# Low parts of the weights in four GpSimd instructions per tile, in every stage

## What is computed

```python
h = _rmsnorm(x, norm_mix)
z = h @ w_in
xr, gr, q, k, v, iq, ik, iw, ga, gb = jnp.split(z, _split_points(), axis=-1)
xc, new_buf = _causal_conv(xr, conv_buf, conv_w, conv_b)
yr, h_last = _rg_lru(xc, h0, w_rg_a, b_rg_a, w_rg_x, b_rg_x, lam)
branch_a = (yr * jax.nn.gelu(gr)) @ w_rnn_out
o = attend(q, k, v, iq, ik, iw)          # top-k keys by the indexer
branch_b = o.reshape(B, T, ATT_W) @ w_att_out
x = x + (jax.nn.sigmoid(ga) * branch_a + jax.nn.sigmoid(gb) * branch_b) @ w_o
h2 = _rmsnorm(x, norm_ffn)
x = x + (jax.nn.silu(h2 @ w_ffn_gate) * (h2 @ w_ffn_up)) @ w_ffn_down
h3 = _rmsnorm(x, norm_ple)
x = x + jax.nn.sigmoid(h3 @ w_ple_gate) * (p_l @ w_ple_proj)
```

## Time and profile before

| | |
|---|---|
| median of three runs | 1089.46 us |
| the profiled execution | 1090.71 us |
| its span, first to last instruction | 1089.0 us |
| TensorE busy | 1038.4 us (95%) |
| VectorE busy | 454.9 us (42%) |
| ScalarE busy | 406.2 us (37%) |
| GpSimd busy | 450.5 us (41%) |
| of it, wlo (line 1512, 213 instructions) | 383.5 us |
| chain that ended last, TensorE's share | 89% |
| mean granted TensorE clock | 0.979 |

### The profile page before, as it was taken

One profiled execution on the slowest core, in us unless ns is written; L12 is line 12 of the kernel. 1 busy time (PEld: TensorE's weight loads), 2 busy tenths in 40 slices (PEclk: granted clock), 3 DMA queues, 4 the chain that ended last, 5 costly groups with the idle time before them and its releaser, 6 DMA issues.

```text
span 1089.0 us, 19209 instructions
## 1 busy us (share of the span) xinstructions
PE 1038.4 (95%) x7847; PEld 977.2 (90%) x7847; DVE 454.9 (42%) x715; ACT 406.2 (37%) x690; POOL 450.5 (41%) x307
## 2 busy tenths in 40 slices
PE   4879999999998999999999899999999999999897
PEld 3867998777897888989999899999999999999796
DVE  3315899487896443423433422222000222212653
ACT  5424233556675443333332622222112222222634
POOL 2613441164665455334441543433444333344540
PEclk9898999999998999999999899999999999999899
DMA  6643265324222312333252323222333232132402
GB/s 181 178 75 90 65 181 152 119 69 145 74 64 77 92 41 69 98 83 94 79 170 69 116 79 96 77 82 68 91 102 104 86 88 69 55 88 80 117 1 82
DMA packets 168750, 101.97 MB, mean 94 GB/s; under 512 B 12626, under 2 KB 160754, under 8 KB 168418
## 3 DMA queue, kind: packets, MB, share of 16 engines
q1 hardware_dynamic: 168674, 100.91, 32.9%
HBM read 93.26 MB, written 7.63 MB: 93 GB/s over the span
## 4 chain that ended last, share of the span: by engine, by line
PE 89%; DVE 4%; ACT 2%; DMA 2%; issue 1%; POOL 1%; SPq 1%; ACTq 0%; DVEq 0%
PE psD L1727 78%; PE psX L1682 2%; DMA wraw<-in_w_in 1%; PE held L1936 1%; PE held L1682 1%; PE psX L1992 1%; PE held L1880 1%; PE psX L1923 1%; PE held L2016 1%; PE psX L1810 1%; DVE h_lo L1063 1%; DMA prm<-in_state_rglru_h 1%; ACT whi L606 1%; DVE hs L1265 0%; DVE xc L1133 0%
## 5 line engine op out<-in xcount | busy, mean ns | idle before, releaser
L1512 POOL TENSOR_TENSOR wlo<-wraw,whi 128x1024 fp32r<-128x1024 f32 (+5 forms) x213 | 383.5, 1812 | 575.8 <-ACT whi L606 575.8
L1727 PE MATMUL psD<-h_hi,whi 128*128 128x272 f32 (+1 forms) x1616 | 348.4, 297 | 13.5 <-DVE h_lo L1063 10.4
L1727 PE MATMUL psD<-h_lo,whi 128*128 128x272 f32 (+1 forms) x1616 | 339.1, 292 | 0.0
L1727 PE MATMUL psD<-h_hi,wlo 128*128 128x272 f32 (+1 forms) x1616 | 339.1, 292 | 0.0
L1727 PEld LDWEIGHTS psD<-h_hi,whi 128*128 128x128 f32 (+1 forms) x1616 | 258.5, 192 | 33.3 <-issue 23.6
L1727 PEld LDWEIGHTS psD<-h_lo,whi 128*128 128x128 f32 (+1 forms) x1616 | 259.3, 192 | 0.0
L606 ACT CAST whi<-wraw 128x1024 fp32r<-128x1024 f32 (+4 forms) x165 | 154.9, 939 | 277.5 <-PE psD L1727 250.2
L1727 PEld LDWEIGHTS psD<-h_hi,wlo 128*128 128x128 f32 (+1 forms) x1616 | 257.3, 192 | 0.0
L1727 PE MATMUL psD<-act_hi,whi 128*128 128x272 f32 x672 | 140.8, 291 | 0.0
L1727 PE MATMUL psD<-act_hi,wlo 128*128 128x272 f32 x672 | 139.1, 288 | 0.0
L1727 PE MATMUL psD<-act_lo,whi 128*128 128x272 f32 x672 | 138.7, 288 | 0.0
(11 more groups left out here) (262 smaller groups left out, 948.6 us busy)
## 6 DMA issues: line engine op xcount, KB each, us to landing
wraw<-in_w_in SPq DMA_DIRECT2D x48, 512.0 KB, 4.9
wraw<-in_w_ffn_gate SPq DMA_DIRECT2D x22, 512.0 KB, 3.7
wraw<-in_w_ffn_up SPq DMA_DIRECT2D x22, 512.0 KB, 3.8
wraw<-in_w_ffn_down SPq DMA_DIRECT2D x16, 384.0 KB, 3.4
wraw<-in_w_ffn_down SPq DMA_DIRECT2D x16, 320.0 KB, 3.2
kpg<-in_cache_k SPq DMA_DIRECT2D x16, 256.0 KB, 3.0
kpg<-in_cache_v SPq DMA_DIRECT2D x16, 256.0 KB, 3.3
wraw<-in_w_rnn_out SPq DMA_DIRECT2D x8, 512.0 KB, 4.8
```

The lines of the kernel that those rows point to most:

```text
L1512: ins = g_.tensor_tensor(wlo[:, s, r0:r1, 0:cc], wraw[:, s, r0:r1, 0:cc], whi[:, s, r0:r1, 0:cc].bitcast(F32), ALU.subtract)
L1727: ins = te.matmul(psD[0:cc, b0 + half, 0:HT], w[:, s, c, 0:cc], m[:, k0 + c, HT * half:HT * (half + 1)], start=(part == 0 and c == 0 and w ...
```

## The change

lower_weights splits a tile's subtraction into four instructions over a quarter of the chunks each, where before it did so for tiles 21 to 36 alone (U["xr"] is 17, U["ga"] is 33, RING is 4) and made one instruction of every other tile. rc is the number of chunks; a tile of two chunks gets two instructions, one of five or six unequal ones. The last of them signals w_lo, as before. No other engine's instructions change.

```diff
                 pool.wait_ge(w_hi, n + 1 + 4 * it)
-                parts = 4 if U["xr"] + RING <= n < U["ga"] + RING else 1
+                parts = min(4, rc)
                 for k in range(parts):
                     r0, r1 = rc * k // parts, rc * (k + 1) // parts
                     ins = g_.tensor_tensor(wlo[:, s, r0:r1, 0:cc], wraw[:, s, r0:r1, 0:cc],
```

## The result

The changed kernel took 1092.44 us (median; 1091.0 to 1094.59), the kernel before, run beside it, 1089.74 us (1087.8 to 1092.05). The ratio is 1.0022, 95% interval 1.0013 to 1.003: 1.4 to 3.3 us slower. The forecast was 1089.8 us with a range up to 1091.7. The profiled execution took 1091.74 us, with a span of 1090.0.

A forecast was written before the change was run, and what follows sets the result against it. TensorE, busy 95% of the span, was taken to bound the kernel. The terms +0.8 + 0.1 - 0.4 - 0.2 = +0.3 us, from the median 1089.46, gave 1089.8 us, range 1088.2 to 1091.7.

The forecast's parts named there:

- start: At 18 to 40 us, tile 2's parts make chunk 5 start 1.6 us late, at half speed: +0.8 us.
- norm before FFN: At 603 to 612 us, the first two h_lo both meet parts and TensorE goes on 0.2 us later: +0.1 us.
- last norm: At 1015 to 1030 us, chunk 2 is ready earlier, 0.4 to 0.6 us pass chunk 3 at half clock: -0.4 us.
- merge: At the end of the merge, act_lo ends earlier and TensorE's 0.26 us wait for it goes: -0.2 us.
- a longer low clock: Rival at the start: TensorE's clock does not come back at 40.1 us, sum 1.9 to 2.3 us; chance 0.12.
- the rival in which it is spared: At the last norm, shorter idle time keeps TensorE's clock up, giving back 2.7 us: 1087.1 us; chance 0.05.
- Attention and FFN: In these stages the chain is TensorE's own and low parts have microseconds of cover: 0 us.
- the price of 0.20 us for each added instruction: On GpSimd, 431 added instructions at 0.20 us fixed cost each: at most 86 us on a largely idle engine.
- GpSimd keeping its turn: Rival at both later norms: VectorE waits for GpSimd's whole queue of parts, costing 2.8 us: 1092.3 us; chance 0.02.

The follow-up runs named there:

- all_two: The changed kernel with tiles cut in two parts instead of four (tiles 21 to 36 stay in four); ratio 0.9993 to the kernel before.
- last_whole: The changed kernel with tiles 157 to 160, under the last norm, formed whole again; ratio 1.0007 to the kernel before.
- norms_whole: The changed kernel with tiles 0 to 3, 77 to 80 and 157 to 160, under the three norms, whole again; ratio 0.9991 to the kernel before.
- last_order: The changed kernel with GpSimd's three h_lo of the last norm moved ahead of tile 160; ratio 0.9994 to the kernel before.
- start_whole: The changed kernel with tiles 0 to 3 formed whole again; ratio 1.0008 to the kernel before.
- only_last: The kernel before with tiles 157 to 160 alone additionally cut in four; ratio 1.001 to the kernel before.
- orders_merge: The kernel before with tiles 21 to 76 cut, GpSimd's h_lo ahead of tile 160 (last norm) and tile 2 (start, chunk 5); 1088.06 us, ratio 0.9978.
- order_uncut: The kernel before, no further cut, with GpSimd's three h_lo of the last norm moved ahead of tile 160; ratio 0.9979 to the kernel before.

## Why the prediction was wrong

The terms of the sum beside the stages: means over the kernels with cut tiles in that place less means over those with whole tiles, the order at the place unchanged; all_two is left out. The profiles of before and after are counted among them.

| term | forecast (bounds) | stages | kernels cut, whole |
|---|---|---|---|
| start | +0.8 (0 to 1.2) | +0.6 to 58 us, +1.0 to 230 us | 4, 7 |
| norm before FFN | +0.1 (-0.3 to 0.7) | +0.16 + 0.27 = +0.4 | 7, 6 |
| last norm | -0.4 (-1.6 to 0.3) | +0.87 - 0.06 = +0.8 | 3, 5 |
| merge | -0.2 (0 to -0.3) | -0.4 | 8, 5 |
| sum | +0.3 | +1.4 to +1.8 | |

With the 1.8 the ratio would be 1.0017, inside the measured interval; the 1.4 are at its lower end, and the 0.3 are outside. Of the middle value, 2.4 us, these stages leave 0.6 to 1.0 us open. The +0.8 of the last norm is the mean of three kernels that lie between +0.18 and +1.30. Another 0.3 us of the miss is the base: 1089.46 was the median of three runs of the kernel before, 1089.74 that of twenty.

**The step that failed is the last norm, and there the rule "at half clock: -0.4 us".** Up to chunk 3 the step was right in kind. I had chunk 2 ready 1.6 us earlier, h_lo of chunk 3 late next, and chunk 3 earlier by 0.4 to 0.6. Against the stage's first matmul, which came 0.68 us earlier in after, chunk 2 came 1.2 us earlier and chunk 3 (1026.86, in before 1027.70, where it started without a wait) 0.16, so that less passed chunk 3 than I had. Timeline of TensorE before, chunk 3:

```profile
1027.70 0.67 PE L1727 MATMUL psD<-h_hi,whi 128*128 128x272 f32 x2
```

I then took the low clock to end where it ended before. It did not. In after TensorE came back from a wait of 0.86 us at 1026.86 and ran without a wait until the clock rose, at 1032.6. Before, its last wait was the 0.40 us ahead of 1026.18, and the clock rose at 1030.0. From chunk 3 on TensorE was at half speed for 5.8 us and not for 2.3, which costs (5.8 - 2.3) / 2 = 1.75 us; less 0.16 this is 1.6, and the stage shows 1.30. Two earlier chunks cannot repay that. I had priced a longer low clock, but as a rival of the start alone; at the last norm I had only the rival in which it is spared. The bound of +0.3 there was too low for the same reason. That sixteen parts lie ahead of h_lo of chunk 3, and not twelve, I had missed in counting on, but the end that I gave for them, 1025.7, is near the 1025.5 measured.

That the longer low clock follows from the wait before chunk 3 is argued from order in time, with support from the runs: without that wait (last_whole, norms_whole, all_two, last_order) it lasted 6.8 us every time; with it 10.2 in after and start_whole, and in only_last 3.4 and 3.4 with a full clock between. No run held all else equal and moved this wait alone. Two figures speak against the wait as the only cause: TensorE's waits in this stage add up to 5.0 us before and 5.1 us after, and orders_merge waits less than order_uncut (3.3 and 4.0 us) and was at half clock for longer (6.8 and 3.4 us). What else decides when the clock falls and rises here stays open.

**The norm before the FFN** was mis-sized. Its mechanism was right (two h_lo 2.35 us; I had 2.0). Again the clock makes the rest: in the seven profiles with cut tiles it was low for 6.8 us each time, in the six with whole tiles three times for 6.8 and three times for 3.4. The kernel before, profiled, was among the long ones, so that my row of it hid what there was to lose.

**The start** was right in mechanism and size: tile 2 4.73 us (I had 4.7, from 30.5 to 35.2), h_lo of chunk 5 1.32 (1.37), chunk 5 1.4 us late (1.6, with 0.2 from tiles 0 and 1 that the trace does not show), and 0.6 to 1.0 us lost (0.8). The clock came back 11.0 to 11.8 us after the stage's first matmul in the four kernels with these tiles cut, 11.4 us after it in the kernel before, as I had assumed. The reason that I gave for its being passed on, TensorE's own order up to 80 us, holds to 58 us. What passes it on from there is another thing: the chain of after shows a load of weights,

```profile
36.19 22.00 PE psD L1727 x162
64.49 15.54 DMA wraw<-in_w_in
```

It stands in SyncE's queue behind a store of VectorE's lines, which TensorE's matmuls of 62 us feed; it lands 15.5 us later and is waited for until 81. The same load takes 15.56 us from 64.32 in before. Whatever is late at 58 us is late at 81; a low clock from 63 to 66.5, which after has and before has not, costs nothing, as TensorE waits for the load anyway. What the stage to 230 us shows beyond the 0.6 goes with the clock behind this wait: it was then low for 6.8 us in all four kernels with cut tiles at the start and in three of the seven with whole ones, for 3.4 us in the other four.

**The merge** gained its whole 0.26 us gap and 0.15 more. **Attention and FFN** were right at 0 (from matmul 1382 to 3691, recurrence and attention, after takes 0.25 us less than before, inside the scatter of 0.9 us between the kernels; from matmul 4218 to 7403 it takes 0.08 us less than before; only_last, whose code there is that of before, 0.76 less, which I cannot explain). Right, too, was the price of 0.20 us for each added instruction: 431 of them made GpSimd busy for 87 us more.

**The rivals.** A longer low clock was what the profile showed, but at the last norm and not at the start. Nowhere was it spared at the last norm; the shortest low stretch was 3.4 us, in order_uncut. GpSimd keeping its turn did not happen, though its 1092.3 us is near the 1092.44 measured: the second h_lo ended at 1021.7 and not behind the parts at 1025.5. A right number from a wrong mechanism.

## What to carry to other kernels

When an engine off the path is in the way of one on it, look first at what it is doing there and whether that work is needed yet: moving one tile behind three small operations was worth 2 us, cutting all tiles in four cost 2.4. A cut into pieces shortens the neighbour's wait, but the pieces' fixed costs and the neighbour's turns push back what stands behind them in the same queue; two pieces can beat four. Lost time in a stage where TensorE's clock has fallen is not to be counted at half speed up to a fixed end: here the end came 3.3 us later, counted from the stage's first matmul, in a stage whose waits added up to the same.

## What the runs showed that I had not expected

- The low clock did not scale with idle time. At the last norm TensorE was at 0.50 for 3.4 us in order_uncut, for 6.8 us in the kernel before and in nine others, and for 10.2 us in after and start_whole, though the stages' waits differ by far less than that from kernel to kernel. A small shift may so be worth over 1 us; no run isolated one.
- The two engines' h_lo get in each other's way as well. In after VectorE's h_lo of chunk 4 met GpSimd's of chunk 3 and took 1.76 us, alone 0.73; GpSimd's of chunk 5 then took 1.85, where one alone took 1.36.
- Beside VectorE a part cost less than I had bounded: sixteen in 13.18 us are 0.82 us each, near the 0.74 of one alone and far from the 1.37 of the recurrence.
